# Attention: probabilities normalised and turned on VectorE in 32x32 blocks, products of values on 32x64 tiles in four banks, and a token order (s, c, y)

## The reference

```python
# group A: 8 query heads, 2 key/value heads of 64, dense over all 512 keys
s = jnp.einsum('bqgrd,bkgd->bgrqk', q_blk, k)
p = jax.nn.softmax(s, axis=-1)
o = jnp.einsum('bgrqk,bkgd->bqgrd', p, v)
# group B: 8 heads, three patterns (window, dilation) = (128,1), (512,4), (2048,16);
# each query sees keys at distances 0, d, 2d, .. up to window/2 on both sides;
# the three outputs are weighted by their softmax denominators,
# which is one softmax over the three patterns' scores together
x = x + concat([a_o, b_o]) @ w_out
```

## Time and profile before

| | |
|---|---|
| median of 3 runs | 1326.79 us (1326.75 to 1327.69) |
| profiled execution | 1325.35 us, of which the span of its instructions is 1323.6 us |
| TensorE (PE) busy | 1295.6 us, 98% of the span |
| TensorE weight loads (PEld) | 1036.3 us, 78% |
| VectorE (DVE) | 542.7 us, 41% |
| ScalarE (ACT) | 542.2 us, 41% |
| GpSimd (POOL) | 639.5 us, 48% |
| a chunk of attention weights, 192 KB | 2.5 us from issue to landing |
| the reload of `x_t` from its copy in memory, 2 MB | 8.4 us from issue to landing |

### The profile page before, as it was taken

The page is one execution under the profiler, slowest core; times in us unless marked ns, Lnnn a source line. Parts: engine busy times, 40 slices in busy tenths (PEclk is TensorE's granted clock), DMA queues, the critical chain, the costliest instruction groups (busy, mean ns, idle before and its releaser), DMA issues.

```text
span 1323.6 us, 18473 instructions
## 1 busy us (share of the span) xinstructions
PE 1295.6 (98%) x6561; PEld 1036.3 (78%) x6561; DVE 542.7 (41%) x860; ACT 542.2 (41%) x998; POOL 639.5 (48%) x513
## 2 busy tenths in 40 slices
PE   8999999999999999999999999998999999999998
PEld 6877777777778888888888877666788888888886
DVE  5366574765635422121302046999652222211021
ACT  4354444444434333333323246785443333333233
POOL 3475563645525444445444444446344444454442
PEclk9999999999999999999999999999999999999999
DMA  6522222122313333333332342325233333333232
GB/s 196 166 72 61 58 70 60 55 66 66 119 54 110 93 96 96 98 99 96 96 97 89 108 152 64 95 73 175 72 86 98 96 95 95 96 118 96 96 96 96
DMA packets 123543, 126.31 MB, mean 95 GB/s; under 512 B 8024, under 2 KB 106584, under 8 KB 122840
## 3 DMA queue, kind: packets, MB, share of 16 engines
q1 hardware_dynamic: 123448, 125.46, 31.6%
q10 hardware_dynamic: 32, 0.01, 0.0%
HBM read 119.15 MB, written 6.29 MB: 95 GB/s over the span
## 4 chain that ended last, share of the span: by engine, by line
PE 57%; issue 21%; POOL 12%; DVE 5%; ACT 3%; DMA 1%; POOLq 0%; SPq 0%; ACTq 0%; DVEq 0%
PE ps L1407 17%; PE ps L1408 16%; PE ps L1409 16%; POOL w_lo L502 12%; PE ps L1814 2%; PE ps L1535 1%; PE ps L1570 1%; PE ps L1547 1%; PE ps L1551 1%; PE ps L1512 1%; POOL rot L511 1%; PE ps L1581 1%; ACT w_hi L564 1%; PE ps L1589 1%; DVE bkn L1122 1%
## 5 line engine op out<-in xcount | busy, mean ns | idle before, releaser
L502 POOL TENSOR_TENSOR w_lo<-w_stage,w_hi 128x512 fp32r<-128x512 f32 (+2 forms) x448 | 572.9, 1284 | 663.1 <-ACT w_hi L564 662.8
L564 ACT ACTIVATE w_hi<-w_stage 128x512 fp32r<-128x512 f32 (+2 forms) x448 | 264.6, 594 | 625.9 <-PE ps L1409 614.7
L1407 PE MATMUL ps<-h_hi,w_hi 128*128 128x512 f32 x1104 | 441.0, 399 | 6.6 <-POOL w_lo L502 2.8
L1409 PE MATMUL ps<-h_hi,w_lo 128*128 128x512 f32 x1104 | 430.7, 390 | 0.0
L1408 PE MATMUL ps<-h_lo,w_hi 128*128 128x512 f32 x1104 | 430.7, 390 | 0.0
L1407 PEld LDWEIGHTS ps<-h_hi,w_hi 128*128 128x128 f32 x1104 | 207.7, 188 | 68.7 <-issue 15.0
L1409 PEld LDWEIGHTS ps<-h_hi,w_lo 128*128 128x128 f32 x1104 | 207.6, 188 | 43.9
L1408 PEld LDWEIGHTS ps<-h_lo,w_hi 128*128 128x128 f32 x1104 | 207.9, 188 | 42.6 <-issue 2.2
L1259 DVE TENSOR_TENSOR silu_g<-ps,rstd_wide 128x512 f32<-128x512 f32 x44 | 30.2, 686 | 327.3 <-PE ps L1409 327.3
L1407 PE MATMUL ps<-w_hi,f_hi 128*128 128x512 f32 x176 | 68.6, 390 | 0.1
L1409 PE MATMUL ps<-w_hi,f_lo 128*128 128x512 f32 x176 | 68.5, 389 | 0.0
(11 more groups left out here) (224 smaller groups left out, 1622.9 us busy)
## 6 DMA issues: line engine op xcount, KB each, us to landing
w_stage<-in_ffn_w_gate_up_dram SPq DMA_DIRECT2D x176, 256.0 KB, 3.1
w_stage<-in_ffn_w_down_dram SPq DMA_DIRECT2D x88, 256.0 KB, 2.7
w_stage<-in_even_w_in_dram SPq DMA_DIRECT2D x96, 192.0 KB, 2.5
w_stage<-in_odd_w_in_dram SPq DMA_DIRECT2D x32, 256.0 KB, 3.0
x_spill<-x_t SPq DMA_DIRECT2D x2, 2048.0 KB, 7.8
x_t<-x_spill SPq DMA_DIRECT2D x2, 2048.0 KB, 8.4
w_stage<-in_odd_w_out_dram SPq DMA_DIRECT2D x16, 256.0 KB, 3.2
w_stage<-in_even_w_out_dram SPq DMA_DIRECT2D x16, 192.0 KB, 2.4
```

The costliest lines, as they stand in the source:

```text
L502: pool.tensor_tensor(out=w_lo[:, s, 0:n], in0=stage[:, s, 0:n], in1=w_hi[:, s, 0:n].bitcast(f32), op=ALU.subtract).then_inc(chunk_lo, 1)
L564: act.activation(w_hi[:, j % RING, 0:n], stage[:, j % RING, 0:n], ACT.Copy).then_inc(chunk_hi, 1)
L1407: pe.matmul(out_, lh, rh, start=start, stop=False, skip_group_check=skip)
L1409: return pe.matmul(out_, ll, rh, start=False, stop=stop, skip_group_check=skip)
```

## The change

- The turns on TensorE and their copies out of the banks are gone. `a_normalise` and `b_normalise` now normalise and then transpose the probabilities in 32x32 blocks on VectorE (`V.transpose`, 128x512 to 128x512, one for each head), into one buffer `pt`. The next exponentials (A) and the mask step after next (B) wait for these.
- In `pt` a quarter of the partitions (32) holds the keys for a quarter of each 128 queries. So the products of values are made on tiles of 32 rows and 64 columns: the quarter a goes into its own bank (1 to 4, for the last pair 0 to 3), with 128 products of 128 columns for A, and 64 of 128 columns and 160 of 32 or 64 columns for B.
- Each quarter needs the values of all keys on its own 32 partitions. So `av` and, for each pair, `bvf` are written to memory and read back four times, once into each quarter (`av_all`, `bvf_all`), by `far_values` on SyncE's queue.
- Scores now share banks with the products (0, 1 against 1 to 4), so they wait for `o_lo_done`, and `v_turn` too, now at j = 2. The tables are new.
- The token order is (s, c, y): token 128s + 4y + c. Loads and stores of x and the views of the recurrent layer follow.
- The output projection goes in groups of 2, 2 and 4 tiles (before 3, 3 and 2); FFN and gates take other banks; the reload of `x_t` is issued at its chunk 20, behind the last products of values.
- `recur(3, ..)` calls `gated(4, 6)` at t = 2 in place of t = 4.

```diff
-WOUT = ([(0, k) for k in range(7)] + [(1, 0), (0, 7)] + [(1, k) for k in range(1, 8)] + [(2, k) for k in range(8)])
-WOUT_TILES = ((0, 1, 2), (3, 4, 5), (6, 7))
-WOUT_BANK = (5, 0, 6)
+WOUT = ([(0, k) for k in range(7)] + [(1, k) for k in range(7)] + [(0, 7), (1, 7)] + [(2, k) for k in range(8)])
+WOUT_TILES = ((0, 1), (2, 3), (4, 5, 6, 7))
+WOUT_BANKS = ((6, 7), (4, 5), (0, 1, 2, 3))
 WOUT_IN = (0, 4, 1, 5, 2, 6, 3, 7)
 C_FFN = [C_WOUT + len(WOUT), 0]
+
+FFN_BANKS = ((4, 5, 6, 7), (0, 1, 2, 3))
...
-A_SCORES = {10: 0, 13: 1, 16: 2, 19: 3}
-A_TURN = {13: 0, 16: 1, 19: 2, 22: 3}
-B_SCORES = {0: 0, 2: 1, 4: 2, 6: 3}
-B_TURN = {3: 0, 5: 1, 8: 2, 10: 3}
-LAST_SCORES = {0: 0, 1: 1, 2: 2, 4: 3}
-LAST_TURN = {2: 0, 3: 1, 5: 2, 7: 3}
-V_TURN = 1
-A_OUT, B_OUT, LAST_OUT = 1, 12, 8
+A_SCORES = {13: 0, 15: 1, 18: 2, 20: 3}
+B_SCORES = {2: 0, 4: 1, 6: 2, 8: 3}
+LAST_SCORES = {2: 0, 5: 1, 8: 2, 11: 3}
+V_TURN = 2
+B_VALUES, LAST_VALUES = 11, 14
+A_OUT, B_OUT, LAST_OUT = 1, 12, 14
+
+
+PV_BANKS, LAST_PV_BANKS = (1, 2, 3, 4), (0, 1, 2, 3)
...
-    tok = 4 * (col % P) + col // P
+    tok = P * (col // P) + 4 * (col % 32) + col % P // 32
...
-        pta = at("pta", Z, [2, NC, T])
+
+
+        pt = at("pt", Z, [2, NC, 16, 32])
         prob_b = at("prob_b", Z + 16 * K, [2, 2, T])
         prob_a = at("prob_a", Z + 24 * K, [2, T])
-        ptf, ptn = at("ptf", Z + 28 * K, [2, 5 * 256]), at("ptn", Z + 38 * K, [2, 2, T])
+        bvf_all, av_all = at("bvf_all", Z + 28 * K, [NC, 5, P]), at("av_all", Z + 38 * K, [NC, NC, P])
...
+        def product(i):
+
+            b0 = (LAST_PV_BANKS if i == 7 else PV_BANKS)[0]
+            return ps[:, b0:b0 + 4, 0:P].rearrange("p a (b i) -> p a b i", b=NC)
+
+        def place(o):
+
+            return o.rearrange("p (b a i) -> p a b i", b=NC, a=4)
+
+        def quarter(a):
+
+            return slice(32 * a, 32 * a + 32)
...
+            def far_values(q, j):
+
+                if j == 10:
+                    sync.wait_ge(v_out0, q + 1)
+                    sync.wait_ge(v_out1, q + 1)
+                    if q:
+                        sync.wait_ge(bvf_all_in, 64 * q)
+                    sync.dma_start(bvf_spill, bvf[:, :, :].rearrange("p j d -> p (j d)")).then_inc(bvf_stored, 16)
+                if j in (12, 13):
+                    sync.wait_ge(bvf_stored, 16 * (q + 1))
+                    sync.wait_ge(pv_done, max(1, 2 * q))
+                    for a in (2 * j - 24, 2 * j - 23):
+                        sync.dma_start(bvf_all[quarter(a), :, :, :].rearrange("p c j d -> p c (j d)"),
+                                       bvf_spill.rearrange("(c x) f -> x c f", c=NC)).then_inc(bvf_all_in, 16)
...
-                if i == 5:
-                    sync.wait_ge(pv_done, 7)
+                far_values(3, i)
+                if i == 20:
+                    sync.wait_ge(pv_done, 8)
                     sync.dma_start(x_t[:, :, :].rearrange("p k t -> p (k t)"), x_spill).then_inc(x_back, 16)
 
...
-            def a_turned(p, c):
-
-                act.wait_ge(turned[0], turns_before_a(p, c) + 1)
-                act.activation(pta[:, 0, :, c * P:(c + 1) * P], ps[:, 2, :].rearrange("p (k q) -> p k q", q=P), ACT.Copy).then_inc(turns_out[0], 1)
...
-                    act.wait_ge(turned[1], turns_before_a(p, c - 1) + 1 if c else turns_before_a(p - 1, 3) + 1)
+                    act.wait_ge(a_turned, 8 * p + 2 * c)
...
-                act.activation(o_hi[:, tile, :], ps[:, 4, :], ACT.Copy).then_inc(o_hi_done, 1)
+                act.activation(place(o_hi[:, tile, :]), product(i), ACT.Copy).then_inc(o_hi_done, 1)
...
-                if i in (10, 11):
-                    square(1, 2 * (i - 10), min(2 * (i - 9), 3), G_FFN)
-                if i in (17, 18):
-                    square(1, 2 * (i - 17) + 3, min(2 * (i - 16) + 3, 6), G_FFN)
+                if i in (19, 20):
+                    square(1, 2 * (i - 19), 2 * (i - 18), G_FFN)
...
+            def turned(hh, c):
+
+                return pt[:, hh, c, :, :].rearrange("p k i -> p (k i)")
+
             def a_normalise(p, c):
 
                 dve.wait_ge(a_exp, 8 * p + 2 * c + 2)
-                step.done(V.reciprocal(a_stat[:, 3, :], a_stat[:, 2, :]))
-                for hh in range(2):
-                    V.tensor_scalar(prob_a[:, hh, :], prob_a[:, hh, :], a_stat[:, 3, hh:hh + 1], None, ALU.mult).then_inc(a_prob, 1)
+                V.reciprocal(a_stat[:, 3, :], a_stat[:, 2, :]).then_inc(a_recip, 1)
+                dve.wait_ge(a_recip, 4 * p + c + 1)
+                V.tensor_scalar(prob_a[:, 0, :], prob_a[:, 0, :], a_stat[:, 3, 0:1], None, ALU.mult).then_inc(a_prob0, 1)
+                V.tensor_scalar(prob_a[:, 1, :], prob_a[:, 1, :], a_stat[:, 3, 1:2], None, ALU.mult).then_inc(a_prob1, 1)
+                if c == 0 and p:
+                    dve.wait_ge(pv_done, 2 * p)
+                elif c == 0:
+                    dve.wait_ge(spilled, 16)
+                dve.wait_ge(a_prob0, 4 * p + c + 1)
+                V.transpose(turned(0, c), prob_a[:, 0, :]).then_inc(a_turned, 1)
+                dve.wait_ge(a_prob1, 4 * p + c + 1)
+                V.transpose(turned(1, c), prob_a[:, 1, :]).then_inc(a_turned, 1)
...
+                V.reciprocal(b_stat[:, b % 2, 3, :], b_stat[:, b % 2, 2, :]).then_inc(b_recip, 1)
+                dve.wait_ge(b_recip, 4 * q + b + 1)
+                for hh, prob_done in enumerate((b_prob0, b_prob1)):
                     prob = prob_b[:, b % 2, hh, :]
-                    V.tensor_scalar(prob, prob, b_stat[:, b % 2, 3, hh:hh + 1], None, ALU.mult).then_inc(b_prob, 1)
+                    V.tensor_scalar(prob, prob, b_stat[:, b % 2, 3, hh:hh + 1], None, ALU.mult).then_inc(prob_done, 1)
+                if b == 0:
+                    dve.wait_ge(pv_done, 2 * q + 1)
+                dve.wait_ge(b_prob0, 4 * q + b + 1)
+                V.transpose(turned(0, b), prob_b[:, b % 2, 0, :]).then_inc(b_turned, 1)
+                dve.wait_ge(b_prob1, 4 * q + b + 1)
+                V.transpose(turned(1, b), prob_b[:, b % 2, 1, :]).then_inc(b_turned, 1)
...
-            def recur(m, between=None):
+            def recur(m, between=None, at_=4):
...
-                    if t == 4 and between is not None:
+                    if t == at_ and between is not None:
...
-            recur(3, lambda: gated(4, 6))
+            recur(3, lambda: gated(4, 6), 2)
...
-                        pe.wait_ge(b_masked, 8 * p)
+                        pe.wait_ge(o_lo_done, 2 * p)
...
+            def a_values(p):
+
+                pe.wait_ge(a_turned, 8 * p + 8)
+                if p == 0:
+                    pe.wait_ge(av_all_in, 64)
                     pe.wait_ge(k_roped, 1)
-                turn_banks_free(turns_before_a(p, c))
-                for hh in range(2):
-                    pe.wait_ge(a_prob, 8 * p + 2 * c + hh + 1)
-                    for k in range(NC):
-                        last = pe.transpose(ps[:, 2 + hh, k * P:(k + 1) * P], prob_a[:, hh, k * P:(k + 1) * P], ident[:, :])
-                    last.then_inc(turned[hh], 1)
-
-            def a_values(p):
-
-                turn_banks_free(turns_before_a(p, 3) + 1)
-                if p:
+                else:
                     pe.wait_ge(o_lo_done, 2 * p)
-                for k in range(NC):
-                    for hh, r in enumerate(heads):
-                        kv = p // 2
-                        last = pe.matmul(ps[r, 4, :], av[:, k, kv * HD:(kv + 1) * HD], pta[:, hh, k, :], start=k == 0, stop=k == NC - 1,
-                                         skip_group_check=True)
+                kv = slice((p // 2) * HD, (p // 2 + 1) * HD)
+                for b in range(16):
+                    for a in range(4):
+                        for hh, r in enumerate(heads):
+                            last = pe.matmul(ps[r, PV_BANKS[a], 0:P], av_all[quarter(a), b % 4, b // 4, kv], pt[quarter(a), hh, :, b, :],
+                                             start=b == 0, stop=b == 15, skip_group_check=True)
...
-                    pe.wait_ge(a_exp, 8 * (q + 1))
+                    pe.wait_ge(o_lo_done, 2 * q + 1)
...
-                turn_banks_free(turns_before_v(q))
+                pe.wait_ge(o_lo_done, 2 * q + 1)
...
+            def far_probabilities(c, hh, j, ck):
+
+                flat = pt[quarter(c), hh, :, :, :].rearrange("p b k i -> p (b k i)")
+                if j == 0:
+                    return flat[:, 32 * ck:32 * ck + 32], slice(0, 32)
+                at_ = 512 * (j - 1) + 32 * (4 + ck)
+                if j == 4:
+                    return flat[:, at_:at_ + 32], slice(96, 128)
+                return flat[:, at_:at_ + 768].rearrange("p (u w) -> p u w", u=2)[:, :, 0:32], slice(32 * (j - 1), 32 * (j + 1))
 
             def b_values(q):
 
-                turn_banks_free(turns_before_b(q, 3) + 1)
+                banks = PV_BANKS if q < 3 else LAST_PV_BANKS
+                pe.wait_ge(b_turned, 8 * q + 8)
                 pe.wait_ge(v_in, 4 * q + 4)
```

(66 more changed lines are left out.)

180 lines of the change are left out of this document (68 added, 112 removed).

## The result

The changed kernel takes 1394.24 us (median of 4, 1391.23 to 1397.38) against 1326.88 (4 runs beside it, 1326.75 to 1327.69): ratio 1.0511, interval 1.0497 to 1.0524. The prediction had 1332.5 us and at most 1358; it had the sign and less than a tenth of the size. The profiled execution's span went from 1323.6 to 1391.2 us, 67.6 more.

A forecast was written before the change was run, and what follows sets the result against it. TensorE bounds the kernel before; after the change VectorE's relay of 6.2 us attention steps sets the pace. Up to the last `a_values` +7.4, last part +3.3, recurrent layer -5.0: +5.7 on 1326.79, 1332.5 us; range 1305 to 1358.

The forecast's parts named there:

- Bank numbers ... and token order, cost nothing: same instructions, same sizes: FFN and gate banks, and token order throughout: the changes were priced at no time.
- `b_values` takes 5.2 (4.0 to 6.3): B products of values on TensorE: 16 near and 40 far rounds take 5.2 us, 1.5 more than before.
- I take 3.6: A products of values on TensorE: 256 rows in 32 rounds at 0.112 us, 3.6 us (4.8 at 0.15).
- Rival 2: Products of values: tiles run four abreast, not eight; `b_values` 12.5, +10.9 us a pair, 1376 us; chance 0.10.
- The recurrent layer. -5.0: `recur(3, ..)`: earlier `gated(4, 6)` removes a 4.1 us `s_lo` wait and 2.9 of slow clock; 2.0 taken back.
- The relay: Attention: scores, VectorE maximum, ScalarE exponentials, VectorE normalising and transposing; 6.2 us steps, 79.3 a pair against 77.3; chance 0.56.
- S: Start of `a_values(p-1)`, from which a pair's times count; first B scores at 8.8 us after it.
- X: A pair's first A scores, 44.6 us after its start; turned A probabilities complete 33.8 us later.
- Transposes: VectorE, two after normalising in each attention step: 0.66 us each.
- rival 3: VectorE's transposes cost like a held two-source operation, 1.3 us, not 0.66: 16 a pair, 1371 us; chance 0.10.
- Rival 1: Attention pairs: TensorE stays the bound, steps under 5.4 us; 1298 us, half hidden 1308; chance 0.24.
- +3.3: Last part, `a_values(3)` to the first FFN product: 67.9 us against 64.6 before.

The follow-up runs named there:

- recur_alone: Kernel before with only `gated(4, 6)` called at step 2 of `recur(3)` in place of step 4: ratio 1.0001.
- late_a: Changed kernel with transfers of x and result split in four, products of values in shorter runs, second A scores before chunk 16, not 15: 1349.69 us.

## Why the prediction was wrong, step by step

- **"Bank numbers ... and token order, cost nothing: same instructions, same sizes"** failed first: 31.0 of the 62 us missing. It compared rows and bytes and not the shape of a transfer, which went from one dimension of 128 rows to 4 x 32. The squares of the four tiles of x had started from 5.5 to 11.2 us; now they start from 9.1 to 25.6, one tile of 512 KB each 5.5 us, on a quarter of the engines, and TensorE waits for each. The views had been taken for a renaming.
- **"`b_values` takes 5.2 (4.0 to 6.3)", "I take 3.6" for `a_values`**: mis-sized, as 9.8 to 10.5 us and 5.2 to 6.3. Over four pairs that is 40.6 for 23.4, the 7.8 of the last part among them, and 23.1 for 14.4: 25.9 us missing. This is also the prediction's own sign of being wrong, "`b_values` over 8". The rate of a burst was right, and the eight tiles run at once. But both bounds were rates of execution; no term asked how fast instructions come. The page of before has a line for their queue (q8, 40 packets, 0.66 MB), which the prediction did not read.
- **Rival 2** (four tiles abreast) and the Trainium skill's floor of 25 ns from start to start (TensorE: Matmul & The Clock Gate, "Wait — 56ns, not 53.3ns?") gave `b_values` 12.5 and 11.2 us, nearer than my sum, and for the wrong reason: the burst runs at 14 ns a row and the far rows at 10.7 (128 of them in 1.59 us, less the last one's own 0.22). The floor does not hold here; the supply comes to 28.9.
- **"The recurrent layer. -5.0"**: measured 0. The wait removed was right; "may slip by 1 to 3 ... I take 2.0 back" is what failed: the seventh chunk waits 4.65 us, and the low clock behind it comes back as well. The prediction had seen that GpSimd would work on in that stretch; it mis-sized what that costs: `s_lo` slipped by 4.2 us in `recur_alone`.
- **The relay** held in time. Less the 1.9 us of `a_values`, B scores start at S+8.6 (8.8 predicted); TensorE waits 1.33 before `b_values` (1.7), 3.75 for `q_f` (4.1), with the lower clock behind it (0.92 to 0.96 over a pair); X to the next S is 33.8 (33.8). With the small products at their predicted lengths the first pair is 85.4 - 1.9 - 4.9 = 78.6 against 79.3. X+33.8 was to be the last turned A probabilities; they were complete at X+33.2 (188.62 to 221.84), and no wait for them stands before `a_values`: TensorE's own chunks and the `q_f` wait took 0.5 longer. That the sum of this half came out is in part luck: two chains ended within 0.6 us of each other, and the one named was not the last. That is why `late_a` gained.
- **Transposes** 0.66 to 0.70 us (0.66 taken): right, and rival 3 falls. Rival 1 falls too: four B steps from 1.4 us behind 147.43 to 173.3 are 6.1 each, not under 5.4.
- **"+3.3" for the last part**: 8.0, of which the last `a_values` (1.6 over its term) and `b_values` (9.8 for 7.8) are 3.6 of the 4.7 missing. The other 1.1: the steps ended 0.8 sooner than predicted, but from 443.8 to 447 the granted clock is 0.50 (0.85 to 450) behind the wait for `o_lo`, and the chunks to the FFN take 26.4 for 24.6.

Sum: 5.7 predicted + 31.0 + 25.9 + 5.0 - 1.4 (from the FFN on; the kernel before with the views alone came out 2.8 shorter between start and tail) = 66.2, measured 67.6. The 1.4 left are the 1.1 of the last part and 0.3 in the pairs.
